# Turning q and k by transposing DMAs instead of on TensorE, with GpSimd taking a quarter of some weight subtractions, in a two-layer encoder

## What is computed

```
h = rms_norm(x);  z = h @ w_in                    # 6656 columns: A q|k|v, B q|k|v, pool channels, three gates
A: 8 query and 2 key heads of 64, rms_norm and axial rotary on q and k, dense attention over all 256 tokens
B: 12 heads of 64 in three groups, rms_norm and rotary on q and k, attention in a dilated window
C: centred mean pooling minus the token, a linear map per group
x = x + (sum_i sigmoid(gate_i) * (branch_i @ w_branch_i)) @ w_out
x = x + (silu(rms_norm(x) @ w_gate) * (rms_norm(x) @ w_up)) @ w_down
```

## Time and profile before

| | |
|---|---|
| median of three runs | 822.84 us |
| the profiled execution: its own time, its span | 823.74 us, 821.9 us |
| TensorE busy | 816.8 us, 99% of the span |
| VectorE, ScalarE, GpSimd busy | 574.0, 436.4, 239.3 us |
| granted TensorE clock | 1.0 over the whole span |
| chain that ended last | 98% TensorE |

### The profile page before, as it was taken

The page is one execution under the profiler, slowest core; times in us unless marked ns, Lnnn a source line. Parts: engine busy times, 40 slices in busy tenths (PEclk is TensorE's granted clock), DMA queues, the critical chain, the costliest instruction groups (busy, mean ns, idle before and its releaser), DMA issues.

```text
span 821.9 us, 9923 instructions
## 1 busy us (share of the span) xinstructions
PE 816.8 (99%) x3884; PEld 667.4 (81%) x3884; DVE 574.0 (70%) x688; ACT 436.4 (53%) x505; POOL 239.3 (29%) x206
## 2 busy tenths in 40 slices
PE   9999999999999999999999999999999999999998
PEld 7887778888888888888888877878888888888886
DVE  5999776667776767664379996677586767666552
ACT  6767755573364454543456686555734544444430
POOL 1342324230023444430023241524200444444200
PEclk9999999999999999999999999999999999999999
DMA  9756687685557676676455467677644566776661
GB/s 343 273 188 179 182 204 203 189 221 171 188 174 230 221 214 200 225 243 215 161 198 203 156 186 198 192 201 204 199 181 177 198 213 224 230 223 206 204 209 43
DMA packets 80142, 165.76 MB, mean 202 GB/s; under 512 B 59840, under 2 KB 60000, under 8 KB 62688
## 3 DMA queue, kind: packets, MB, share of 16 engines
q1 hardware_dynamic: 78176, 158.88, 61.3%
q0 software_dynamic: 1632, 6.18, 2.2%
q10 hardware_dynamic: 288, 0.08, 0.0%
HBM read 149.91 MB, written 1.05 MB: 184 GB/s over the span
## 4 chain that ended last, share of the span: by engine, by line
PE 98%; DMA 1%; DVE 0%; ACT 0%; SPq 0%; issue 0%
PE bank L1036 30%; PE bank L1038 30%; PE bank L1047 30%; PE bank L1069 2%; PE bank L1163 2%; PE bank L1140 1%; PE bank L1131 1%; PE bank L1104 1%; DMA x_sb<-in_x_dram 1%; PE bank L1110 0%; DVE w_lo L755 0%; PE bank L1173 0%; ACT w_hi L591 0%; ACT aT_hi L601 0%; DVE scratch L779 0%; DVE x_sb L931 0%
## 5 line engine op out<-in xcount | busy, mean ns | idle before, releaser
L755 DVE TENSOR_TENSOR w_lo<-w_raw,w_hi 128x2048 fp32r<-128x2048 f32 x134 | 317.8, 2374 | 97.5 <-ACT w_hi L591 97.1
L591 ACT ACTIVATE w_hi<-w_raw 128x2048 fp32r<-128x2048 f32 x134 | 256.3, 1915 | 155.5 <-DMA w_raw<-in_stream_dram 155.3
L1036 PE MATMUL bank<-w_hi,aT_hi 128*128 128x512 f32 x832 | 330.3, 397 | 0.0
L1038 PE MATMUL bank<-w_hi,aT_lo 128*128 128x512 f32 x832 | 324.7, 390 | 0.0
L1047 PE MATMUL bank<-w_lo,aT_hi 128*128 128x512 f32 x832 | 223.6, 391 | 0.1
L1036 PEld LDWEIGHTS bank<-w_hi,aT_hi 128*128 128x128 f32 x832 | 156.4, 188 | 37.3 <-issue 5.7
L1047 PEld LDWEIGHTS bank<-w_lo,aT_hi 128*128 128x128 f32 x832 | 155.6, 188 | 33.1 <-DVE w_lo L755 0.7
L1038 PEld LDWEIGHTS bank<-w_hi,aT_lo 128*128 128x128 f32 x832 | 156.6, 188 | 31.4
L539 POOL COPY hT_raw<-turned 128x512 uint16<-128x512 uint16 x44 | 35.6, 853 | 135.1 <-DMA turned<-halves 135.1
L530 POOL COPY halves<-hid 128x512 uint16<-128x512 uint16 x44 | 71.8, 1660 | 4.5 <-DVE hid L1008 4.5
L1036 PE MATMUL bank<-w_hi,hT_hi 128*128 128x512 f32 x176 | 68.7, 390 | 0.0
(11 more groups left out here) (98 smaller groups left out, 745.4 us busy)
## 6 DMA issues: line engine op xcount, KB each, us to landing
w_raw<-in_stream_dram SPq DMA_DIRECT2D x135, 1024.0 KB, 4.8
bias_sb<-in_b_gate_dram POOLq DMA_DIRECT2D x12, 256.0 KB, 3.5
par<-in_params_dram POOLq DMA_DIRECT2D x3, 384.0 KB, 3.5
w_raw<-in_stream_dram SPq DMA_DIRECT2D x4, 256.0 KB, 5.3
pool_mat<-in_pooling_dram POOLq DMA_DIRECT2D x1, 1024.0 KB, 7.5
out_dram<-x_sb SPq DMA_DIRECT2D x4, 256.0 KB, 4.2
x_sb<-in_x_dram SPq DMA_DIRECT2D x2, 256.0 KB, 4.1
x_sb<-in_x_dram SPq DMA_DIRECT2D x1, 512.0 KB, 6.3
```

Source lines behind the costliest of these rows:

```text
L591: nc.scalar.activation(w_hi[:, j % RING, :, :].rearrange("p k n -> p (k n)"), w_raw[:, j % RING, :, :].rearrange("p k n -> p (k n)"), ACT. ...
L755: nc.vector.tensor_tensor(w[0], w[1], w[2].bitcast(F32), ALU.subtract).then_inc(unit_lo, 1)
L1036: nc.tensor.matmul(o, src[0][:, k, tok], w_hi[:, slot, wk + i, :], start=first and i == 0, stop=False)
L1038: nc.tensor.matmul(o, src[1][:, k, tok], w_hi[:, slot, wk + i, :], start=False, stop=False)
```

## The change

Two things change, both within units 2 to 17 of each layer.

First, the transposes of q and k leave TensorE. ScalarE separates the 16-bit halves of each region and token half (`split_heads`, two slots after `rotate`), SyncE issues one transposing DMA for each after the load of unit t+4 (`turn_heads`), and the halves are joined into `qkT`: branch A's q and k by ScalarE in slots 7 and 8, branch B's by GpSimd in slots 13 to 16. TensorE waits for `heads_joined` before the scores of pair 0 and for `late_heads_joined` before those of pair 4.

Second, for units 4 to 14 the subtraction that gives `w_lo` is divided: VectorE does three k-tiles, GpSimd the fourth, in its slot t for unit t+2.

```diff
+JOIN_UNITS = (7, 8, 13, 14, 15, 16)
-    6: [("qk", 0)], 7: [("qk", 2)],
-    0: [("mix_x", 2), ("mix_x", 3)], 6: [("qk", 1)],
-    10: [("qk", 3)], 11: [("qk", 4)], 12: [("qk", 5)], 13: [("qk", 6)], 14: [("qk", 7)], 15: [("qk", 8)],
+    0: [("mix_x", 2), ("mix_x", 3)],
+HEAD_TILES = [(0, 4), (4, 1), (5, 2), (7, 4), (11, 4), (15, 2)]
+SHARED = range(4, 15)
+KEPT = UK - 1
...
 @block.sync
+            def turn_heads(lay, r, m):
+                sp.wait_ge(heads_split, lay * TURNED + (MT * r + m + 1))
+                sp.dma_start_transpose(turned_room(r, m).rearrange("p (g t) -> p g t", t=P), split_room(r, m)
+                                       ).then_inc(heads_turned[r], 16)
...
+                for n in range(TURNED):
+                    if lay >= 0 and REGIONS[n // MT][-1][n % MT] == t - 2:
+                        turn_heads(lay, *divmod(n, MT))
                 if lay >= 0 and pair_at(t, 1) is not None:
                     turn_probs(lay, pair_at(t, 1))
...
 @block.gpsimd
+            def split_last_tile(lay, j):
+                pool.wait_ge(unit_hi, lay * (UNITS - 1) + j)
+                w = [a[:, j % RING, KEPT, :] for a in (w_lo, w_raw, w_hi)]
+                nc.gpsimd.tensor_tensor(w[0], w[1], w[2].bitcast(F32), ALU.subtract).then_inc(last_tile_lo, 1)
+            def join_heads(lay, r, m):
+                pool.wait_ge(heads_turned[r], (lay + 1) * 16 * MT)
+                nc.gpsimd.tensor_copy(joined_heads(r, m), turned_heads(r, m)).then_inc(late_heads_joined, 1)
...
+                    if t + 2 in SHARED:
+                        split_last_tile(lay, t + 2)
                     for n in range(TURNED):
                         if REGIONS[n // MT][-1][n % MT] == t:
                             head_norm(lay, n)
+                    for r in range(2, len(REGIONS)):
+                        if JOIN_UNITS[r] == t:
+                            for m in range(MT):
+                                join_heads(lay, r, m)
...
 @block.scalar
+            def split_heads(lay, n):
+                r, m = divmod(n, MT)
+                first, k = HEAD_TILES[r]
+                act.wait_ge(rotated, lay * TURNED + (n + 1))
+                both = zqk[:, m, P * first:P * (first + k)].bitcast(U16).rearrange("p (f h) -> p h f", h=2)
+                nc.scalar.activation(split_room(r, m).rearrange("p (h f) -> p h f", h=2), both, ACT.Copy
+                                     ).then_inc(heads_split, 1)
+            def join_heads(lay, r, m):
+                act.wait_ge(heads_turned[r], (lay + 1) * 16 * MT)
+                nc.scalar.activation(joined_heads(r, m), turned_heads(r, m), ACT.Copy).then_inc(heads_joined, 1)
...
                     for j in splits_at(t, ahead=3):
                         split(lay, j)
+                    for n in range(TURNED):
+                        if REGIONS[n // MT][-1][n % MT] == t - 2:
+                            split_heads(lay, n)
+                    for r in range(2):
+                        if JOIN_UNITS[r] == t:
+                            for m in range(MT):
+                                join_heads(lay, r, m)
...
 @block.vector
-                w = [a[:, j % RING, :, :].rearrange("p k n -> p (k n)") for a in (w_lo, w_raw, w_hi)]
+                k = KEPT if j in SHARED else UK
+                w = [a[:, j % RING, 0:k, :].rearrange("p k n -> p (k n)") for a in (w_lo, w_raw, w_hi)]
...
 @block.tensor
+                    if opening and t in SHARED and i == KEPT:
+                        pe.wait_ge(last_tile_lo, lay * len(SHARED) + SHARED.index(t) + 1)
...
                 if p == 0:
-                    wait_emptied(pe, lay, ("qk", 2))
+                    pe.wait_ge(heads_joined, lay * 4 + 4)
                 if p == 4:
-                    wait_emptied(pe, lay, ("qk", 7))
-                    wait_emptied(pe, lay, ("qk", 8))
+                    pe.wait_ge(late_heads_joined, lay * 8 + 8)
```

More of the change, by code:

```diff
@@ L131, in turns_within @@
     return TURNS_WITHIN.get(t, [])
-QK_BATCH = [(0, 2), (2, 2), (4, 1), (5, 2), (7, 2), (9, 2), (11, 2), (13, 2), (15, 2)]
+HEAD_TILES = [(0, 4), (4, 1), (5, 2), (7, 4), (11, 4), (15, 2)]
 SCALED = ("mix_x", "mixed", "ffn_x")
 SPLIT = ("o", "merged", "hidden")
-PLAIN = ("qk", "pool")
+PLAIN = ("pool",)
 X_BANKS = (4, 0)
@@ L252, in build @@
         pool_mat = sb("pool_mat", [P, MT, POOL_G, SEQ])
+        with ExitStack() as shared:
+            head_halves = sb("head_halves", [P, 20 * MT * 2 * P], U16, shared)
         mixT_hi = sb("mixT_hi", [P, POOL_G, SEQ], F32R)
@@ L301, in build @@
         unit_lo = sem("unit_lo")
+        last_tile_lo = sem("last_tile_lo")
         first_hi = sem("first_hi")
@@ L326, in build @@
         hidden_ready = sem("hidden_ready")
+        heads_split = sem("heads_split")
+        heads_turned = [sem(f"heads_turned{r}") for r in range(len(REGIONS))]
+        heads_joined = sem("heads_joined")
+        late_heads_joined = sem("late_heads_joined")
         vchain = sem("vchain")
@@ L403, in probs_part, with split_room, turned_room, turned_heads @@
             return probs[:, i % 2, :]
+        def split_room(r, m):
+            first, k = HEAD_TILES[r]
+            at = 2 * P * (MT * ((first + 8) % 19) + m * k)
+            return head_halves[:, at:at + 2 * P * k]
+        def turned_room(r, m):
+            first, k = HEAD_TILES[r]
+            return zqk[:, m, P * first:P * (first + k)].bitcast(U16)
+        def turned_heads(r, m):
+            return turned_room(r, m).rearrange("p (h k t) -> p h k t", h=2, t=P)
+        def joined_heads(r, m):
+            first, k = HEAD_TILES[r]
+            return qkT[:, first:first + k, P * m:P * m + P].bitcast(U16).rearrange("p k (t h) -> p h k t", h=2)
         block = ctx.enter_context(nc.Block())
@@ L599, in turn @@
                     wait_emptied(act, lay, name)
+                    if name == ("mixed", 0):
+                        act.wait_ge(late_heads_joined, lay * 8 + 8)
                     src = scratch[:, NC * (n % 2):NC * (n % 2) + NC]
@@ L612, in turn @@
                                          ).then_inc(turn_hi, 1)
[L613 to L616, removed]
-                else:
+                else:
+                    if i == 0:
+                        act.wait_ge(late_heads_joined, lay * 8 + 4)
                     free(nc.scalar.activation(pooledT[:, 2 * i:2 * i + 2, :].rearrange("p k n -> p (k n)"),
@@ L1088, in transposes @@
                         last = turn(P * k, merged[:, m, P * (UK * half + k):P * (UK * half + k + 1)])
[L1089 to L1096, removed]
                 elif kind == "pool":
```

## The result

The changed kernel takes **844.36 us** (median of 4 runs, 841.13 to 847.84); the kernel before took 823.17 beside it (4 runs, 822.70 to 823.88). The ratio is 1.0257 [1.0213, 1.0302]: 2.6% slower, where 820.7 us and a gain were forecast. The profiled execution took 841.13 us itself, the fastest of the four, with a span of 839.3 against 821.9.

A forecast was written before the change was run, and what follows sets the result against it. TensorE, busy 99% of the span, was taken to bound the kernel. Removed transposes (-4.08 us a layer) plus waits gave -1.4 and -0.8, together -2.2 us: median 820.7, range 815.0 to 827.0.

The forecast's parts named there:

- Hidden or small: Loads, SyncE's issues, split_heads on ScalarE and GpSimd's late joins: hidden or already priced, except 0.2 us a layer for joins.
- The chains above: Dependency chains to TensorE's waits at unit 9 (0.6 and 1.2 us) and unit 12 (1.9 us in each layer).
- The gain, -8.16 us: TensorE without its transpose batches saves 4.08 us a layer, 8.16 in two, if it never waits.
- GpSimd's subtraction, 1.2 us and a loss of 0.85: GpSimd's fourth k-tile takes 1.2 us and costs VectorE 1.2 x 0.8 x 0.88 = 0.85, against 0.53 gained.
- rival C: Each GpSimd subtraction costs VectorE 1.2 us or more, deciding from about 1.0; units 9 and 12 wait longer: 827; chance 0.18.
- Unit 9, 0.6 and 1.2: TensorE waits before unit 9's scores for ScalarE's joins: 0.6 us in layer 0, 1.2 in layer 1.
- Unit 12, 1.9 each: TensorE waits before unit 12 for ScalarE to copy out z5 of half 0: 1.9 us in each layer.
- Unit 17, 0.2 each: GpSimd's last joins of B's keys delay unit 17 by 0 to 0.8 us; 0.2 taken in each layer.

The follow-up runs named there:

- variant with both orders: Changed kernel with every w_lo subtraction on VectorE, branch A's k joined first in slot 8 and z7 copied out first in slot 15: 819.31 us.
- the division alone: Kernel before with only the divided w_lo subtraction added, q and k still transposed on TensorE: 827.14 us.
- changed kernel with both orders: Changed kernel, GpSimd's subtraction kept, with A's k joined first in slot 8 and z7 copied out first in slot 15: 828.64 us.
- z7 first: Changed kernel with one edit, VectorE copying z7 out of its banks at the start of slot 15: 827.64 us.
- the subtraction given back: Changed kernel with all of every w_lo subtraction back on VectorE, DMA transposes and joins as they were: 835.24 us.
- z7 first on that base: Changed kernel with every w_lo subtraction back on VectorE and z7 copied out at the start of slot 15: 819.94 us.

## Why the prediction was wrong

**The step that failed** is the list of what could be late. "Hidden or small" put `split_heads` at "some 9 us a layer", said "its price is in the chains above", and looked at GpSimd's joins only for the last scores. The chains above were those of units 9 and 12. The forecast did not follow `split_heads` of the last regions on: it waits for VectorE in slot 14, ScalarE's split and exponentials queue behind it, VectorE's divisions wait for these, and z7's copy stands behind the divisions. And it put at nothing what GpSimd's joins take from VectorE, 6.4 us in slot 13 (8.4 for 2.0), which makes the first hand-over late. Either one removed takes most of the wait away: z7's copy moved, all of it; VectorE ahead of the joins, all but 1.0 us a layer. Each hand-over is plain in the order of instructions; the forecast followed each change to its first customer and not round to the bank. This is 16.7 of the 23.7 us missed by the medians, or 13.7 of 19.6 by the profiled executions: 70% either way.

**The gain, -8.16 us:** right in the main. The variant with both orders has one wait that the kernel before lacks, 0.9 us, and a span of 816.2; 821.9 - 8.2 + 0.9 = 814.6, so 1.6 us of it is missing there. That execution was one of the fastest of its six: by the medians 4.2 us are gained, and 3.1 are missing. Where they are isn't known.

**GpSimd's subtraction, 1.2 us and a loss of 0.85:** the duration was near (it takes 1.29 where nothing holds it), the loss too small where it counts. It was multiplied by 0.8 and by 0.88 as though the operation fell anywhere in the slot. Where it starts on the signal that starts VectorE's split, it meets the next multiplication, 1.10 us each time in seven of eleven slots; in slots 9 and 11 it costs nothing. The five ahead of unit 9's chain cost 0.5 + 4 x 1.10 = 4.9 us, where 4.25 was forecast. 1.10 lies past the 1.0 from which rival C was to decide.

The Trainium skill (SBUF — State Buffer, "Who interferes with whom") calls the shared port pair an exclusive lock, and says that the first to issue holds it for the whole instruction where it speaks of VectorE's two-port modes; for two inputs it says only that the engines contend, which the prediction ran together. The trace is nearer to the whole instruction than to my 0.8: 1.10 of 1.29.

**Unit 9, 0.6 and 1.2:** 2.33 and 2.99. In layer 0 the large joins were to start at 53.25 us and started at 54.49: the first half of B's q was rotated 0.7 us late, and the sum had left out its second half's own `split_heads`, 0.56. The joins took 1.21 start to start, not 0.95 (+0.5 for two), the two small ones with the hand-over to TensorE 0.3 more. In layer 1 the loss to GpSimd is most of it: 0.74 us without the subtraction. A join moved to the head of the slot removes both waits.

**Unit 12, 1.9 each:** 0.33 in layer 0 of the changed kernel, 1.70 in layer 1. The mechanism was right: 2.05 and 1.68 with the division alone, 3.06 and 4.50 with the other waits gone. From the end of unit 9 the bank came 12.66 us later in layer 0 (69.54 to 82.20) and 14.03 in layer 1 (482.74 to 496.77), where 13.0 and 1 us more were forecast. What the sum had wrong is that it treated the two waits as separate. In layer 0 the bank came at 82.20 us, and at 82.47 with the wait at unit 9 gone: what TensorE doesn't wait at unit 9 it waits at unit 12. Both together are 2.66 and 4.69 us in the changed kernel, 3.06 and 4.74 in the changed kernel with both orders, where 2.5 and 3.1 were forecast; so layer 1 is what was mis-sized, by 1.6.

**Unit 17, 0.2 each:** not shown. No run has a wait before the first scores of unit 17. The waits for the probabilities' joins that come up when unit 16's is gone (up to 1.9 us with z7 first) stand at 173 to 187 us and their like in layer 1, outside the stretch of the change; nobody followed them.

**The clock** was in no term. After the waits of 7.11 and 5.84 us, and in the variants after 4.50, 3.06 and 2.05, the next matmuls ran 0.43 us apart, each time at a cost of 1.3 to 2.6 us by their starts. After 2.33 and 2.99 us at unit 9 of the changed kernel they ran 0.23 apart. And after nearly the same wait at the same place, 2.16 us with the subtraction given back and 2.17 with z7 first on that base, they ran 0.23 apart in the one and 0.43 in the other. So the length of the wait isn't all that decides; what else does is open.

## What to carry to other kernels

Follow every instruction that is put into a full queue round the whole loop, past its first customer, until the bank or buffer comes free that TensorE needs next; a wait nobody listed was 70% of this miss. Put the instruction that frees a bank ahead of work that itself waits for another engine: here the place of two copies was worth 15 us, more than the removed transposes. And where two operations are released by one signal, look at what stands next on each engine: here they collided in seven of eleven slots at the full price and in two at none, which an average over the slot hides.

## What the runs showed of the hardware that was not expected

- GpSimd's fill with zeros, 0.52 us for 128x512 float32, ran inside VectorE's two-input subtraction, and neither was held (1.75 us). GpSimd's subtraction of the same shape, 1.29 us by itself, took 2.80 from the same start.
- Also VectorE's division of one tensor by a scalar per partition (128x256) was held off by copies on GpSimd, 1.3 to 1.4 us instead of 0.31 (slot 13), and 16-bit copies of GpSimd are held in turn: four took 5.55 us in one order and 9.23 in the other.
- ScalarE's 16-bit copy of 1024 elements takes 1.06 us on the mean when it reads with a stride (`split_heads`) and 1.35 when it writes with one (`join_heads`).
- A load of a megabyte with a region's transposes issued behind it landed after 6.1 us in the changed kernel and 7.8 in one variant, where the earlier trace rows has 5.9.
